# Pass 0 of a gated pooling and convolution block: fold steps moved ahead of a convolution chunk, weight copies moved to GpSimd's queue and spread over two passes

## The reference

```
shift, scale, gate = split(W_ada silu(c) + b_ada)
h = RMSNorm(x) * (1 + scale) + shift
z = h W_in + b_in -> [a_v | a_g | b_B | b_C | b_v | b_g | m_A | m_B]     (8 x 1024 columns)
y_A = gamma * GroupLinear(TrailingMeans(a_v) - a_v) * silu(a_g)           (4 groups of 256 channels)
y_B = b_B * CausalConv3(b_C * b_v) * silu(b_g)
o = (sigmoid(m_A) * (y_A W_A) + sigmoid(m_B) * (y_B W_B)) W_o
out = RMSNorm(x + gate * o) * final_g
```

## Time and profile before

| | us |
|---|---|
| median of 3 runs (2530.87 to 2531.14) | 2531.1 |
| the profiled execution | 2530.9 |
| its span, slowest core (core 5; the others 2521.9 to 2528.3) | 2529.3 |
| PE busy | 2466.8 |
| DVE / ACT / POOL busy | 1295.0 / 739.4 / 185.2 |

### The profile page before, as it was taken

The page is one execution under the profiler, slowest core; times in us unless marked ns, Lnnn a source line. Parts: engine busy times, 40 slices in busy tenths (PEclk is TensorE's granted clock), DMA queues, the critical chain, the costliest instruction groups (busy, mean ns, idle before and its releaser), DMA issues.

```text
span 2529.3 us, 32709 instructions; the slowest of 8 cores (2521.9 to 2529.3 us)
## 1 busy us (share of the span) xinstructions
PE 2466.8 (98%) x11552; PEld 1121.5 (44%) x11552; DVE 1295.0 (51%) x1421; ACT 739.4 (29%) x795; POOL 185.2 (7%) x238
## 2 busy tenths in 40 slices
PE   5899899999999999999999999999999999999997
PEld 2444344444444444444444444444444444444443
DVE  4654335563456544664346644566335563446524
ACT  3224123332332223332233222333223322222212
POOL 3111111110000100001000110000000010000000
PEclk9999999999999999999999999999999999999999
DMA  9947986865334563344423473244533346323341
GB/s 242 176 92 129 227 179 144 187 168 187 95 93 150 154 172 95 113 134 151 145 84 109 146 198 124 86 129 128 179 102 93 125 147 183 94 77 113 110 140 67
DMA packets 149791, 345.70 MB, mean 137 GB/s; under 512 B 17656, under 2 KB 17784, under 8 KB 149632
## 3 DMA queue, kind: packets, MB, share of 16 engines
q1 hardware_dynamic: 127168, 300.79, 37.8%
q0 software_dynamic: 22032, 42.48, 11.4%
q10 hardware_dynamic: 432, 0.35, 0.1%
HBM read 331.45 MB, written 54.56 MB: 153 GB/s over the span
## 4 chain that ended last, share of the span: by engine, by line
PE 95%; DMA 2%; DVE 1%; issue 1%; ACT 0%; SPq 0%; POOL 0%; DVEq 0%; ACTq 0%; POOLq 0%
PE ps_z L386 86%; PE ps_z L864 8%; DMA sb_t<-x 1%; DMA wb<-sb_wsl 1%; PE ps_z L534 0%; DMA sb_wsl<-ws 0%; DVE sb_t L739 0%; DVE sb_hT L598 0%; PE ps_z L518 0%; PE ps_z L587 0%; SPq L426 0%; DVE sb_yb L502 0%; DVE sb_t L732 0%; DVE sb_t L735 0%; SPq L849 0%
## 5 line engine op out<-in xcount | busy, mean ns | idle before, releaser
L386 PE MATMUL ps_z<-sb_hT,sb_wsl 128*128 128x512 bf16 x8000 | 1756.2, 379 | 0.0
L386 PEld LDWEIGHTS ps_z<-sb_hT,sb_wsl 128*128 128x128 bf16 x8000 | 782.8, 98 | 943.9
L829 DVE TENSOR_TENSOR sb_t<-ps_z,sb_t 128x1024 f32<-128x1024 f32 x64 | 78.4, 1225 | 347.6 <-ACT sb_t L826 344.6
L386 PE MATMUL ps_z<-sb_ya,sb_wsl 128*128 128x512 bf16 x1024 | 233.8, 382 | 6.6 <-DMA sb_wsl<-ws 6.6
L386 PE MATMUL ps_z<-sb_yb,sb_wsl 128*128 128x512 bf16 x1024 | 231.5, 379 | 0.0
L864 PE MATMUL ps_z<-sb_wo,sb_mg 128*128 128x512 bf16 x1008 | 227.0, 379 | 1.0 <-DVE sb_mg L837 1.0
L417 POOL TENSOR_TENSOR sb_nwt<-sb_nwt,sb_mhalf 128x1 f32<-128x1 f32 x62 | 77.3, 1246 | 1818.7 <-DVE sb_nwt L414 1002.7
L718 DVE SCALAR_TENSOR_TENSOR sb_v<-ps_z,sb_cvec,sb_t 128x1024 f32<-128x1024 f32 x64 | 82.2, 1285 | 221.3 <-PE ps_z L386 218.9
L817 DVE TENSOR_TENSOR sb_t<-ps_z,sb_t 128x1024 f32<-128x1024 f32 x64 | 78.4, 1225 | 201.2 <-ACT sb_t L814 195.5
L826 ACT ACTIVATE sb_t<-ps_z,sb_cvec 128x1024 f32<-128x1024 f32 x64 | 71.3, 1114 | 351.2 <-PE ps_z L386 351.1
L725 ACT ACTIVATE sb_t<-ps_z,sb_cvec 128x1024 f32<-128x1024 f32 x64 | 71.3, 1114 | 320.8 <-PE ps_z L386 320.7
(11 more groups left out here) (116 smaller groups left out, 1352.0 us busy)
## 6 DMA issues: line engine op xcount, KB each, us to landing
sb_wsl<-wb SPq DMA_DIRECT2D x520, 256.0 KB, 2.7
sb_xn<-x SPq DMA_DIRECT2D x64, 512.0 KB, 7.2
y<-sb_xn SPq DMA_DIRECT2D x60, 512.0 KB, 3.0
sb_xt<-x SPq DMA_DIRECT2D x56, 512.0 KB, 5.6
sb_wsl<-ws POOLq DMA_DIRECT2D x112, 256.0 KB, 7.3
sb_xf<-xT SPq DMA_DIRECT2D x56, 512.0 KB, 5.2
wb<-sb_wsl SPq DMA_DIRECT2D x72, 256.0 KB, 7.0
sb_wo<-wo POOLq DMA_DIRECT2D x32, 256.0 KB, 7.5
```

The lines of the kernel that those rows point to most:

```text
L386: ins = e.matmul(Z[zb][:, sblk * 512:(sblk + 1) * 512], w[:, k, :], src[:, k, sblk * 512:(sblk + 1) * 512], start=(k == 0), stop=(k == 7))
L829: P.op("dve", lambda e: e.tensor_tensor(out=t2[:], in0=Z[zob][:], in1=t2[:], op=ALU.mult), reads=[bZ[zob], bT2[ti]], writes=[bT2[ti]])
```

## The change

Three edits.

1. `steps(0)`: the fold of group 3 is still behind conv 1, but conv 2 now comes between it and pool 6. The folds of groups 2, 1 and 0 come behind the even pool step of the group ahead (pool 6, 4, 2), and ahead of a conv chunk; every conv step is one place earlier. The main loop calls a fold that stands behind a pool step before it calls the conv step.
2. `late` holds the first 16 tiles of conv and pool steps (which with the new order are conv 0 to 3) and the 16 merge tiles with odd index. So pass 0 copies tiles 16 to 39 and the merge tiles of even steps (16), 40 in all; pass 1 copies 32, and loads 32 from the f32 input where it was 40.
3. The copies of `keep_w` are issued by POOL and not by SP.

```
@@ steps
-                out = conv[0:2]
+                out = conv[0:2] + [("fold", 3), conv[2]]
                 for i, c in enumerate((6, 7, 4, 5, 2, 3, 0, 1)):
-                    if i % 2 == 0:
-                        out.append(("fold", c // 2))
                     out.append(pool[c])
-                    out += conv[i + 2:i + 3]
+                    if i in (0, 2, 4):
+                        out.append(("fold", 2 - i // 2))
+                    out += conv[i + 3:i + 4]
@@ build_nc
-        late = set(w for w in order if w[0] == "z" and w[1] < 48)
+        branch = [w for w in order if w[0] == "z" and w[1] < 48]
+        late = set(branch[0:16] + [w for w in order if w not in branch and w[1] % 2 == 1])
@@ keep_w
-            P.dma("sp", "k%d" % slot,
+            P.dma("pool", "k%d" % slot,
@@ the main loop
+                if si < len(seq) and seq[si][0] == "fold":
+                    fold(seq[si][1])
+                    si += 1
                 if si < len(seq) and seq[si][0] == "conv":
                     conv_chunk(p, seq[si][1], hooks=pending)
```

## The result

| | before | after |
|---|---|---|
| median of the fast runs, one chip (us) | 2531.1 | **2578.6** |
| ratio, 95% interval | | 1.0187 [1.0169, 1.0204] |
| profiled execution: time / span (us) | 2530.9 / 2529.3 | 2580.5 / 2579.0 |
| first tail product (us) | 381.04 | 430.70 |

The account below looks back on a forecast made before the run. PE, busy 98% of the span, bounds the kernel now; after the change POOL's round trips per copied tile would end pass 0 at 390.7 instead of 360.3, so 2531.1 + 30.4 = 2561 us, range 2517 to 2604.

Parts of the forecast that it names:

- After that as before: Fifth sign for the new profile: from the first tail product, forecast at about 411 us, everything stays as before.
- first turn ends: Pass 0, POOL's queue: copy 16, issued at 112.6, stands behind a slow load; its round trip ends at about 124 us.
- 15 turns to tile 39: Pass 0, tiles 24 to 39: part of the copies of tiles 17 to 39, each one POOL round trip of 5.5 us.
- W_o pairs and norm, to tile 47: Pass 0: W_o adds four single round trips on POOL at 6.7 each, 26.8 us, before tile 47's load is issued at 277.3.
- four turns of the merge step, 47 to 51: Pass 0 merge steps: four copies on POOL at 7.1 us each, 28.4 us, between tiles 47 and 51.
- issue and landing of tile 51's load: Pass 0: 4.6 us for a load to land and 0.5 of issue, in the sum that puts tile 51 at 310.8.
- tile 51 to the end of pass 0: PE's chunk and 20 more (72.5), 1.6 at lower clock, 5.8 for two copied groups; pass 0 ends at 390.7.
- 23 further copies at 5.5: Pass 0, tiles 17 to 39: each copy costs POOL one round trip of 5.5 us, 126.5 us together.
- B: Rival: round trips of 6.1, then 9 in the merge steps; pass 0 ends 69 us later, 2600 to 2616; chance 0.18.
- C: Rival: round trips of 4.6 to 4.8, 5.5 in merge; pass 0 ends 10.9 us faster, run at 2520; chance 0.16.
- the fold's 17 us: Pass 0: moving the folds ahead of other chunks removes PE's waits behind them, about 17 of 17.8 us.

## Why the forecast was right, and where it was 19 short

Point by point, by its own expectations:

1. *No gap behind the folds but about 1 us, clock 1.00 in 75 to 220.* Right: 0.78, and 1.00 up to 200; in 200 to 220 it is 0.80, as the starving begins at 205 already. A wait of 1.74 for a tile at 115.67 wasn't forecast.
2. *Loads some 5.5 apart from 124 on, each behind a copy.* Right. The first turn ends at 125.4. Of the 15 turns from tile 24 to tile 39, thirteen average 5.52.
3. *35 to 50 us of waits for tiles between 220 and 310.* In that stretch they are 36.0. In all they are 59.8, with the 1.7 at 115, 8.8 at 205 and 216, and 13.2 after it, up to 393: the mechanism, for longer.
4. *First tail product at 411.* It is 430.7. This is the miss.
5. *After that as before.* Right.

The terms of the sum, measured on the same core:

| term | forecast | measured |
|---|---|---|
| first turn ends | 124 | 125.4 (+1.4) |
| 15 turns to tile 39 | 15 x 5.5 | 13 x 5.52, and 15.5 and 11.2 (+16.0) |
| W_o pairs and norm, to tile 47 | 26.8 | 27.4 (+0.6) |
| four turns of the merge step, 47 to 51 | 28.4 | 29.6 (+1.2) |
| issue and landing of tile 51's load | 5.1 | 5.4 (+0.3) |
| tile 51 to the end of pass 0 | 79.9 | 79.6 (-0.3) |

The mis-sized term is "23 further copies at 5.5", which took that duration for all of them. Two turns fell where x, xT and folded weights come in on SP. The row for this stood in the earlier trace rows: a W_o trip among x tiles took 10.8 where its neighbours took 4.6 to 7.2. I gave that row to the W_o term alone, and took a middle value there, though in the changed kernel W_o comes after the x tiles (224.52) and the copies meet them instead. With 10.8 for two turns and 6.0 for each W_o trip, the mean of the other three, the sum would have been 10.6 - 2.8 = 7.8 longer and the forecast 2569. That two turns would be hit is known only now, and a turn of 15.5 against 10.8 no row of before showed. What makes the first of them long stays open.

Part of the miss belongs to the core. On the mean of the eight cores the first tail product comes 45.9 us later than before (377.9 and 423.8), not 49.7. The first long turn is there on every core, but it took 7.9 to 12.1 on the other seven, with two or three others over 6.5 beside it; the 15 turns take 93.8 on the mean, 11 more than 82.5.

The agreement of the third row is partly luck: of its 27.4 the four W_o trips are 24.8, where the forecast had 26.8, and the norm's operation, which had no term, is 1.6.

Of the rivals, B (deeper, 2600 to 2616) had merge turns of 9; they are 7.4 in the first group and 5.9 in the run with the queue alone. C needed turns of 4.6 to 4.8, and 5.5 in the merge steps; the shortest turn to tile 39 on any core is 5.22. The price from the Trainium skill ("DMA: Bandwidth & Descriptors", section "Anatomy of one DMA — SWDGE (gpsimd) path"), 2.0 us and the bytes over 436 GB/s, gave an estimate of 4.9 for a load and a copy. The trace shows 5.25 to 5.46 in quiet, and the measurement decides. That difference alone does not turn the loss into a gain: with 4.9 in place of 5.5 and the other terms as they are, the sum is 13.8 less, 2547, and the gain of C needed short W_o trips and merge turns besides. What the same section says of a write to HBM, the longest confirmation, these traces can't tell, since in this stretch each copy stands behind a load: in the change such a copy lands 4.3 us after its issue and a load 4.1 (110 to 180 us, medians, loads first):

```profile
DMA to landing us min/median/max: 4.0/4.1/13.1
```
```profile
DMA to landing us min/median/max: 4.1/4.3/13.3
```

The sum runs along POOL's queue and so gives the fold's 17 us no term. The run without the folds bears that out: 3 to 5 us apart.

## What to carry to other kernels

Where a load waits for the landing of a copy issued just ahead of it on the same in-order queue, each tile costs one full round trip, also with the DMA engines half idle (share 0.43 to 0.52 in 120 to 180): here 5.5 us a tile against 3.45 of use. The changed kernel was 47 us slower than before, and with one tile of lead 14 us faster. Put a write-back in an in-order queue well ahead of the instruction that waits for it; then the choice of queue mattered little here (2507.7 and 2508.8). And count the whole queue: a forecast of the turns needs the duration of each kind of stretch, the ones with foreign traffic too, and a gain ahead of a starved stretch is no gain.

## What the runs showed of the hardware

- The turn on GpSimd's queue is very even in quiet stretches: 5.25 to 5.46 us for the seven from 147.64 to 184.98.
- Where tiles of x and xT and folded weights come in on SP's queue such turns took 15.5 and 11.2 us, with the DMA engines nearly full (share 0.96 in 190 to 200, 0.82 over the second turn, 207.0 to 217.7). Without the x tiles the second was gone and the first was not.
- Two W_o loads issued together ahead of a copy, without a wait between them: the copy landed 6.4 us after its issue, where it was 4.5 behind a single one that came after a wait.
- Cores 0 to 3 ran at a granted clock of 0.97 and cores 4 to 7 at 1.00 with a full PE (500 to 700 us), in one kernel whose pass 1 had other data. Why is open.
